# State-space scan: two band products in one accumulation in place of their sum on GpSimd

## The reference, cut to what matters

```
def _s5_bidirectional(u, lam_re, lam_im, log_dt, b_re, b_im, c_re, c_im, d_skip):
    ...
    for direction, reverse in ((0, False), (1, True)):
        ...
        lam_bar = jnp.exp(lam * dt)
        b_bar = ((lam_bar - 1.0) / lam)[..., None] * b
        c = lax.complex(c_re[direction].astype(jnp.float32), c_im[direction].astype(jnp.float32))
        bu = jnp.einsum('sbgh,gph->sbgp', u_c, b_bar)
        a = jnp.broadcast_to(lam_bar, (seq, 1, SSM_GROUPS, SSM_STATE))
        _, h = lax.associative_scan(_diag_scan_op, (a, bu), reverse=reverse, axis=0)
        y = y + jnp.real(jnp.einsum('sbgp,ghp->sbgh', h, c))
    y = y + d_skip.astype(jnp.float32).reshape(SSM_GROUPS, SSM_GROUP_CH) * u_t
```

## Time and profile before

| what | value |
|---|---|
| median of three runs | 4457.07 us (4455.8 to 4459.76) |
| the profiled execution's own time | 4459.97 us |
| its span in the trace | 4458.1 us |
| PE busy, share of the span | 4035.8 us, 91% |
| DVE busy | 2951.5 us, 66% |
| ACT busy | 2430.3 us, 55% |
| POOL busy | 1346.0 us, 30% |
| mean of the DMA engines' traffic | 163 GB/s |
| stage `s5` in the trace | about 1185 to 1415 us |

### The profile page before, as it was taken

How to read it: one execution, slowest core, us unless ns; L and a number is a source line. 1 busy time by engine, 2 the same in 40 slices (tenths; PEclk the granted TensorE clock), 3 DMA queues, 4 the chain that set the end, 5 groups by cost and what they waited for, 6 DMA issues and landing times. The chain is left out here.

```text
span 4458.1 us, 61305 instructions
## 1 busy us (share of the span) xinstructions
PE 4035.8 (91%) x21541; PEld 3424.1 (77%) x21541; DVE 2951.5 (66%) x3768; ACT 2430.3 (55%) x3867; POOL 1346.0 (30%) x874
## 2 busy tenths in 40 slices
PE   8989799999785997999799999997599699999985
PEld 8978688888674886888677777776588588888872
DVE  6667555555476775444477667764655799999975
ACT  6633333333212554333378888887522477777763
POOL 0000244444310000000189999995000121222123
PEclk9999899999898998999889999998799799999997
DMA  6667723333576333222250000002643588888986
GB/s 225 215 210 249 231 91 113 122 106 106 168 216 201 118 111 121 67 75 70 74 191 15 15 15 15 22 10 85 234 147 130 197 321 316 324 316 332 382 321 261
DMA packets 417338, 728.63 MB, mean 163 GB/s; under 512 B 121744, under 2 KB 314385, under 8 KB 396305
## 3 DMA queue, kind: packets, MB, share of 16 engines
q1 hardware_dynamic: 387648, 662.08, 43.4%
q10 hardware_dynamic: 15552, 30.81, 2.2%
q0 software_dynamic: 13968, 33.58, 2.0%
HBM read 603.93 MB, written 213.91 MB: 183 GB/s over the span
## 5 line engine op out<-in xcount | busy, mean ns | idle before, releaser
L2637 POOL TENSOR_TENSOR a_PL<-a_PT,a_PH 128x512 fp32r<-128x512 f32 x576 | 762.1, 1346 | 68.5 <-ACT a_PH L2753 67.0
L2798 DVE TENSOR_REDUCE a_part<-a_pA 128x1 f32<-128x1024 f32 (+1 forms) x384 | 367.0, 958 | 244.0 <-PE a_pA L2660 241.1
L3420 POOL DMA_INDIRECT w_XG<-between_h,all_slots x65 | 188.6, 2902 | 712.0 <-PE e_pT L3708 654.2
L2751 ACT ACTIVATE a_PT<-a_pB 128x512 f32<-128x512 f32 x576 | 340.9, 592 | 98.0 <-PE a_pB L2683 96.6
L2753 ACT ACTIVATE a_PH<-a_PT 128x512 fp32r<-128x512 f32 x576 | 364.2, 632 | 18.3
L1391 ACT ACTIVATE a_PT<-a_pT 128x512 f32<-128x512 f32 x128 | 69.6, 594 | 408.8 <-PE a_pT L1321 408.7
L1426 DVE TENSOR_REDUCE a_maxima<-a_pS 128x1 f32<-128x512 f32 x256 | 176.3, 689 | 131.2 <-PE a_pS L1303 129.8
L1233 POOL TENSOR_TENSOR a_QL<-a_RQ,a_QT 128x512 fp32r<-128x512 f32 x16 | 20.5, 1281 | 800.6 <-DVE a_QP L1461 800.6
L2621 POOL MEMSET a_QA<- 64x1024 f32 x2 | 1.8, 944 | 828.1 <-POOLq L2178 828.1
L1335 PE MATMUL a_pO<-a_V,a_PT 128*128 128x128 f32 x2048 | 250.4, 275 | 1.0 <-DVE a_PT L1439 1.0
L1335 PEld LDWEIGHTS a_pO<-a_V,a_PT 128*128 128x128 f32 x2048 | 244.2, 192 | 6.5 <-DVE a_PT L1439 1.2
(11 more groups left out here) (624 smaller groups left out, 10742.1 us busy)
## 6 DMA issues: line engine op xcount, KB each, us to landing
w_gate<-in_moe_w_gate SPq DMA_DIRECT2D x48, 2048.0 KB, 7.5
w_up<-in_moe_w_up SPq DMA_DIRECT2D x47, 2048.0 KB, 11.8
w_down<-in_moe_w_down SPq DMA_DIRECT2D x46, 2048.0 KB
between_yb<-e_Y SPq DMA_DIRECT2D x45, 512.0 KB, 7.1
a_row_w<-in_w_ada SPq DMA_DIRECT2D x16, 1024.0 KB, 5.4
between_x<-m_X SPq DMA_DIRECT2D x32, 512.0 KB, 2.9
between_yb<-a_zeros SPq DMA_DIRECT2D x32, 512.0 KB, 14.4
between_tv<-pz_OV SPq DMA_DIRECT2D x16, 576.0 KB, 2.9
```

What stands on the lines that cost most here:

```text
L2637: pool.tensor_tensor(PL[:, t % RING, :], PT[:, t % RING, :], PH[:, t % RING, :].bitcast(F32), ALU.subtract).then_inc(S["p_low"], 1)
L2751: act.activation(PT[:, t % RING, :], pB[t % 2][:], ACT.Exp, scale=scale).then_inc(S["p_ready"], 1)
L2798: dve.tensor_reduce(part[:, h, r % (NG2 // G4):r % (NG2 // G4) + 1], src, AX_X, ALU.max).then_inc(S["maxed"], 1)
```

## The change

`LL` and the semaphore `L_ready` are gone. POOL keeps only `with_skip`. PE multiplies `X` by `LF` and by `LB`, one after the other into the same accumulation, so that a group has six products. PE now waits for the bands' DMAs itself. SP, before it overwrites a pair of bands, waits until PE has done all outputs of the turn that read them (`y_ps`), and no longer for POOL's sum.

```
-        LF, LB, LL = ([k.sb(f"{n}{b}", [P, HG, P]) for b in range(2)] for n in ("LF", "LB", "LL"))
+        LF, LB = ([k.sb(f"{n}{b}", [P, HG, P]) for b in range(2)] for n in ("LF", "LB"))
...
-            def both_bands(h):
-                b = h % 2
-                pool.wait_ge(L_dma[b], 32 * T8 * (h // 2 + 1))
-                if h >= 2:
-                    pool.wait_ge(S["y_ps"], 2 * (h - 1))
-                pool.tensor_tensor(LL[b][:], LF[b][:], LB[b][:], ALU.add).then_inc(S["L_ready"], 1)
-
             for h in range(TURNS):
                 with_skip(h)
-                both_bands(h)
...
                 if h >= 2:
-                    sp.wait_ge(S["L_ready"], h - 1)
+                    sp.wait_ge(S["y_ps"], 2 * (h - 1))
                 sp.wait_ge(S["k_ready"], h + 1)
...
                 if 0 in groups:
-                    pe.wait_ge(S["L_ready"], h + 1)
+                    pe.wait_ge(L_dma[b], 32 * T8 * (h // 2 + 1))
                     pe.wait_ge(S["products_1"], h + 1)
                     pe.wait_ge(S["products_2"], h + 1)
...
-                    pe.matmul(y, LL[b][:, g, :], X[r][:, g, :], start=True, stop=False)
+                    pe.matmul(y, LF[b][:, g, :], X[r][:, g, :], start=True, stop=False)
+                    pe.matmul(y, LB[b][:, g, :], X[r][:, g, :], start=False, stop=False)
```

More of the change, by code:

```diff
@@ L1576, in s5 @@
         pY = [k.ps(f"pY{b}") for b in range(2)]
-        names = """d_loaded zeroed w_ps w_moved L_ready s_ps turned summed scanned products_1 products_2 y_ps y_moved skip_ready k_ready""".split()
+        names = """d_loaded zeroed w_ps w_moved s_ps turned summed scanned products_1 products_2 y_ps y_moved skip_ready k_ready""".split()
         S = {n: k.sem(n) for n in names}
```

## The result

| | before | changed |
|---|---|---|
| median, 8 runs each | 4456.91 us (4453.61 to 4464.29) | 4477.77 us (4468.89 to 4480.66) |
| profiled execution, its span | 4459.97, 4458.1 us | 4478.26, 4476.5 us |
| stage s5 in that trace, first engine instruction to ACT's last | 226.1 us | 237.9 us |

The ratio is 1.0042, interval 1.0031 to 1.0052: slower by 14 to 23 us. The forecast was 4470 us (+13.2), the range 4464 to 4476. The direction and the mechanism held, and the stage grew by what was forecast; the whole did by more. By the ratio, 4457.07 us become 4475.8, just inside the range; the bare median of the changed kernel, 4477.8, lies 2 us above it.

The account below looks back on a forecast made before the run. The prediction took a circle of waves, PE, weight copies and wave transfer to bound the stage. Added work of 8.8 us and clock falls of 4.4 us gave +13.2 us on 4457.07: 4470 us, range 4464 to 4476.

Parts of the forecast that it names:

- outputs of turn 0: First outputs on PE: start 0.92 us sooner, added matmuls cost 0.88 and 1.29 us; together +1.25 us.
- outputs of turns 1 to 5: Added matmuls of groups 1 to 3 lie in the circle, 1.29 us a turn, +6.45 us; group 0's is free.
- transfers of six waves: Time from ACT's request for the waves to DVE's use, 8.4 us in the steady turn, stays as it is.
- DVE's turn 7: Last turn: four added matmuls count, +1.72 us; DVE's sum without POOL beside it gives -1.01 us.
- The circle: Steady turn of 23.9 us: waves, 10.8 us of PE, 4.7 of preparing and copying, 8.4 of transfer.
- DVE's gain: Scans 1.05 us faster a turn without POOL's sum; hidden in DVE's wait for waves, counted once, -1.01 us in turn 7.
- The clock: PE's two pauses become one of 2.8 us; two of four turns fall to half clock at 2.2 us: +4.4 us.
- The rest of the program: Stages behind s5: no term was forecast, so the stage's +13.2 us was taken for the whole program.
- The clock as before: Rival: PE's clock stays as it is, so +8.8 us, 4465.9 us; chance 0.25.
- Every turn cold: Rival: PE starts every turn at half clock, +20.4 us, 4477.5 us; chance 0.05.
- Hidden matmuls: Rival: waves' arrival depends on DMA load, not request time, hiding 6.45 us: +2.4 us, 4459.5 us; chance 0.05.
- a faster kernel: Rival: bands' DMAs leave the waves' way, waves land in 5.2 us: -10.4 us, 4446.7 us; chance 0.03.

Follow-up runs that it names:

- e6: Kernel before, with ACT asking for the next turn's waves ahead of its copies of the weights: ratio 0.9965, s5 212.1 us.
- e9: e6 with the next stage's weights loaded behind the outputs of turn 6 instead of turn 4: ratio 0.9949, s5 206.7 us.
- e10: e9 with the outputs of groups 0 and 1 ahead of states 4 to 7: ratio 0.9949, s5 206.6 us.
- e11: Kernel before, with four idle products on PE in its second pause, behind outputs(h, 0): ratio 1.0004, s5 225.9 us.
- e4: Changed kernel with the bands' sum put back on GpSimd, its result unused and PE not waiting for it: ratio 1.0035, s5 239.1 us.
- e8: Changed kernel with five idle products on PE behind outputs(h, 0), in its single pause: ratio 1.0035, s5 244.6 us.
- e5: Changed kernel with the outputs of group 1 moved ahead of states 4 and 5: ratio 1.0000, s5 224.4 us.
- e7: Changed kernel with ACT asking for the waves ahead of its copies of the weights: ratio 0.9971, s5 214.5 us.

## Why the prediction was right and where it was wrong

By its own steps, with the two traces of the change against the first trace of before. The prediction numbers the added matmuls by the turn of their outputs; the outputs of turn h run while DVE works on turn h+1, so its turns 1 to 5 are PE's part of turns 2 to 6 above.

| step | predicted | first trace | second trace |
|---|---|---|---|
| up to the first waves waited for (two scans) | 0 | +0.1 | -0.05 |
| outputs of turn 0: start sooner, one product at half clock, three at full | +1.25 | -0.36 | +1.21 |
| outputs of turns 1 to 5: PE's part of the circle, clock included | +6.45 and some falls | +8.93 | +9.24 |
| transfers of six waves | 0 | -0.2 | +1.0 |
| DVE's turn 7, from its waves to the end | +1.14 and a fall | +3.32 | +3.37 |
| s5 | +13.2 | +11.8 | +14.8 |
| stages behind it | 0 | +5.9 | +7.0 |

**The circle** (waves, PE, weights, waves) was right: transfers kept their length, each turn grew by what was added on PE, and group 0's matmul was free in its pause. 16.76 - 15.47 = 1.29 us is the predicted term to the hundredth.

**Turn 0** was right where the clock rose about as before (+1.21, second trace). In the first trace it rose sooner, and that gave 1.6 us back. PE in order of time, the changed kernel's first trace:

```profile
1223.65 1.19 PE L1725 MATMUL s_pY<-s_X,s_LF 128*128 128x256 f32 x2 [4.63 <-DVE s_SIN L1808]
...
1225.49 1.06 PE L1727 MATMUL s_pY<-s_COS,s_TV 128*128 128x255 f32 x2
1226.34 0.69 PE L1728 MATMUL s_pY<-s_SIN,s_TU 128*128 128x255 f32 x2
1226.86 0.59 PE L1729 MATMUL s_pY<-s_COS,s_TV 128*128 128x255 f32 x2
```

The products are at full cadence some 2.7 us behind PE's start, where before they were some 4.9 us behind it (1224.19, and 0.89 still at 1228.60).

**DVE's gain** stayed in its wait, as forecast (5.4 to 6.4 us of wait in turns 2 to 5 of the first trace, where 5.5 was named), and came out once, in turn 7: L1800 took 2.29 us at 1398.19, and no POOL instruction stands beside it.

```profile
1398.19 2.29 DVE L1800 TENSOR_TENSOR s_R<-s_R 128x2048 f32<-128x2048 f32 x1
```

**The clock** came to the forecast sum with other parts. "I take two of four at 2.2 us: +4.4" became three of four, turns 3, 4 and 7, in both traces: 1.69 us each in turns 3 and 4 (a fall was priced at 2.2) and, in turn 7, 3.32 - 1.14 = 2.2, together 5.6 us. Of the 2.2, 1.7 are the fall behind the waves; 0.5 lie in the stage's last outputs, which begin at half clock in both kernels (1.19 us for the first product) and so pay more than 0.43 us for the sixth. The prediction had priced this at full clock. Turn 6 gave some back: it was cold before and after, but lost 0.9 and 0.8 us less (18.83 and 18.98 us, where 18.45 + 1.29 = 19.74 would be no change), and turn 0 gave back 1.6 us in the first trace and nothing in the second. Net some 3 and 5 us, against 4.4. That the sum fits is in part luck: one fall more than assumed, each of them cheaper, and a gain in turns 0 and 6 that was not forecast. The pauses were 2.8 to 3.8 us in turns 2 to 5 and 7 of the first trace, where 2.8 was computed; they are longer where the waves took longer (3.79 us with 9.17 us of transfer, 2.82 with 8.20). The mechanism, two pauses joined into one, was right. What I had missed is that the removal of the sum does this by itself: I priced the faster DVE at nothing in the turns ("the gain goes into that wait"), and put the fall of the clock down to the order of waits as a whole. The sum-off experiment shows 7.2 us for it without any matmul added. In the change's sum the price was counted, in that of the removal it was not.

**The rest of the program** is the step that failed. The forecast for the stage, 13.2 us, is the mean of what the two traces show (11.8 and 14.8, mean 13.3), and I took it for the whole: nothing was to change behind the stage. In both traces of the change the stages behind s5 took longer, by 5.9 and 7.0 us, and with them the first comparison makes sense (14 to 23 us). The later runs tell how far that is the change's doing. Their traces give for the time behind s5, from ACT's last output to the last instruction of DVE, in us (the 6.5 us behind the stage that the expectations name are what the whole span leaves, and hold what lies ahead of the stage too):

| kernels | traces | mean |
|---|---|---|
| within-chunk term from the summed bands (before, again, e6, e9, e10, e11) | 3038.7, 3039.9, 3039.1, 3039.0, 3043.9, 3041.0 | 3040.3 |
| from separate bands (change, again, e4, e8, e5, e7) | 3044.6, 3045.7, 3034.0, 3042.5, 3042.5, 3038.7 | 3041.3 |

The means differ by 1.0 us and each row scatters by 5 to 12 us, so most of the 5.9 and 7.0 us is not owed to the changed values or to the changed stage as such: e4 has both, and is the shortest of all. The comparisons of whole runs say the same with less weight on one trace: 9 to 21 us for the change again, 10 to 21 for e4 with the same work on PE, and the stage's 13.3 us lies in both, just below the first interval. In the other four kernels with separate bands (e4, e8, e5, e7) the medians differ from before by 12.2, 17.5, -1.0 and -11.7 us and s5 by 13.0, 18.5, -1.7 and -11.6: the stage accounts for the whole within 1 us. In the change it leaves 9.1 us in the first run and 3.4 in the second. Inside the rest there may be more: the stage of experts took 842.2 us in the mean of the first row and 845.8 in the second, and the mixing stage ahead of it 312.4 and 310.6 us. Two differences of opposite sign picked out of many stages show nothing yet. Whether the change costs something behind its stage, and why the median of eight runs came out 2 us above a range that fits the stage, stays open.

**The rivals.** The clock as before (+8.8) lies below both intervals. Every turn cold, +20.4 or 4477.5 us, lies inside the first interval and within 0.3 us of the median, but that is chance and not its mechanism: turn 5 was warm twice, and s5 grew by 11.8 and 14.8 us. Hidden matmuls and a faster kernel fell: the turns did grow, and the waves were used as long after their request as before (8.2 to 9.2 us in turns 2 to 5 of the first trace, 8.2 to 8.6 before), though the bands' DMAs now start 3.0 us behind the waves' and not 2.7. The Trainium skill's rule in "TensorE: Matmul & The Clock Gate", section "HAM oscillation — how this bites in real kernels", that a DMA wait between bursts puts TensorE back to half rate round after round, agrees with the trace of the change in turns 2, 3, 4 and 7 (PEclk 0.64 to 0.67 over the 3.4 to 3.7 us behind the pause) and not in turn 5 (1.00), where before it held in turns 2 and 6. The Trainium skill's rule on the shared ports, in "SBUF — State Buffer", section "SBUF: two separate sides", agrees in the scans of 4.77 us without a sum on GpSimd and 5.72 with one.

## What to carry to other kernels

Find the circle before pricing an edit: here it ran through a DMA request that stood behind its engine's copies, which wait for PE, so a matmul cost 0.43 us on one side of a wait and nothing on the other, and moving the request gave 14 us while removing some 14 us of GpSimd work gave none. Taking work off an engine with spare time is not always harmless: it can join two short pauses of TensorE into one long one and cost its clock; look at where the idle time lies, not only how much there is. And when a schedule changes, price the same edit anew: the added matmuls cost 12 to 15 us in the old order and 2 in the new one.

## What the runs showed that I had not expected

- Removing work alone made the kernel slower: ratio 1.0022 (1.0013 to 1.0031), with pauses of 1.47 and 1.80 us turned into 0.45 and 2.7 to 3.0.
- The clock falls came in the same turns in both traces of the change. Turns 2 and 5 have pauses of one length, and PE's rows behind them read alike at first, but behind the first PEclk is 0.67 and behind the second 1.00:

```profile
1252.58 0.70 PE L1711 MATMUL s_pX<-s_X,s_WB 128*128 128x256 f32 x2 [2.82 <-DVE s_R L1798]
...
1254.12 1.06 PE L1712 MATMUL s_pX<-s_X,s_WB 128*128 128x256 f32 x2
...
1334.07 0.70 PE L1711 MATMUL s_pX<-s_X,s_WB 128*128 128x256 f32 x2 [2.82 <-DVE s_R L1798]
...
1335.47 0.59 PE L1712 MATMUL s_pX<-s_X,s_WB 128*128 128x256 f32 x2
```

  The length of the pause alone does not decide (in the second trace 2.72 us was followed by a fall, in turn 3, and 2.87 was not, in turn 5), and the fall shows some 1.5 us behind the first product (1252.58 to 1254.12). What decides was not found.
- In turns 2 to 5 the second half of the waves (`SIN`) mostly landed 7.6 to 8.4 us after its request, and in some 8.7 to 10.4, as in turn 2 of the second trace of the change (used 10.71 us after the request for `COS`). With PE busy through the wait both were seen (7.6 to 8.2 in the kernel before with idle products, 8.9 to 10.4 in the changed one), so PE's work alone is not the cause; what is, was not found.
